# A fused two-block model on one core: attention takes its context pieces and its x pieces in turn

## The reference

```python
s = jnp.einsum('bikgd,bjkd->bkgij', q, kc).astype(jnp.float32) * (A_HEAD_DIM ** -0.5)
p = jax.nn.softmax(jnp.concatenate([sink_l, s], axis=-1), axis=-1).astype(vc.dtype)
return jnp.einsum('bkgij,bjkd->bikgd', p[..., 1:], vc).reshape(B, lc, A_WIDTH)
```

```python
s_loc = jnp.where(valid, s_loc, -jnp.inf)
s_ctx = jnp.einsum('bikgd,bjkd->bkgij', q_n, kc).astype(jnp.float32) * scale
p = jax.nn.softmax(jnp.concatenate([sink_l, s_ctx, s_loc], axis=-1), axis=-1).astype(v.dtype)
```

## Time and profile before

| what | value |
|---|---|
| median of 3 runs | 1845.88 us (1842.76 to 1850.29) |
| the profiled execution: time, span | 1848.1 us, 1845.4 us |
| TensorE (matmul), VectorE, ScalarE, GpSimd busy | 84%, 45%, 20%, 10% of the span |
| attention: first scores, first matmul of the output projection | 1312.58, 1383.15 us |
| granted TensorE clock in attention from 1319 us on | 1.00 |
| transfers in flight in attention, 1315 to 1380 us | share 0.00 to 0.01 |

### The profile page before, as it was taken

One profiled execution on the slowest core, in us unless ns is written; L12 is line 12 of the kernel. 1 busy time (PEld: TensorE's weight loads), 2 busy tenths in 40 slices (PEclk: granted clock), 3 DMA queues, 4 the chain that ended last, 5 costly groups with the idle time before them and its releaser, 6 DMA issues. The chain is left out here.

```text
span 1845.4 us, 19291 instructions
## 1 busy us (share of the span) xinstructions
PE 1555.1 (84%) x7431; PEld 933.9 (51%) x7431; DVE 826.0 (45%) x1536; ACT 371.3 (20%) x702; POOL 193.0 (10%) x282
## 2 busy tenths in 40 slices
PE   4999972689999799476799859999889799999877
PEld 2877662688444444242334325444564456646563
DVE  2344549344344377442112133355664325555553
ACT  3212153111101100110001010100450134622230
POOL 0000027300000000001000000000450001202330
PEclk8899976668999899678899979999899899999887
DMA  9221002210877476669999974252300221131101
GB/s 353 79 91 46 1 1 46 53 27 4 306 244 270 175 279 219 233 254 417 416 395 365 389 263 170 91 182 69 137 1 23 91 91 46 46 136 47 47 1 46
DMA packets 126745, 283.72 MB, mean 154 GB/s; under 512 B 28568, under 2 KB 30904, under 8 KB 121403
## 3 DMA queue, kind: packets, MB, share of 16 engines
q1 hardware_dynamic: 123056, 266.78, 39.5%
q0 software_dynamic: 3600, 15.73, 2.1%
HBM read 312.90 MB, written 4.19 MB: 172 GB/s over the span
## 5 line engine op out<-in xcount | busy, mean ns | idle before, releaser
L2245 PE MATMUL ps<-hT,ring 128*128 128x512 f32 x400 | 176.4, 600 | 0.3 <-issue 0.3
L1312 PE MATMUL ps<-ring,hTx 128*128 128x512 f32 x320 | 139.2, 593 | 1.9 <-PEq L178 1.8
L2245 PEld LDWEIGHTS ps<-hT,ring 128*128 128x128 f32 x400 | 76.7, 192 | 95.7 <-issue 95.5
L2588 PE MATMUL ps<-hT,ring 128*128 128x512 f32 x256 | 113.5, 600 | 3.1 <-PEq L2495 2.7
L299 DVE SCALAR_TENSOR_TENSOR ada_acc<-ring,cact,ada_acc 128x512 f32<-128x512 f32 x154 | 104.1, 746 | 0.5
L1312 PEld LDWEIGHTS ps<-ring,hTx 128*128 128x128 f32 x320 | 60.4, 190 | 77.1 <-issue 77.1
L603 PE MATMUL ps<-hTx,ring 128*128 128x256 f32 x384 | 90.9, 392 | 5.3 <-PEq L178 5.3
L2095 PE MATMUL ps<-ring,hT 128*128 128x512 f32 x192 | 86.4, 611 | 2.6 <-PEq L178 2.4
L603 PEld LDWEIGHTS ps<-hTx,ring 128*128 128x128 f32 x384 | 74.6, 197 | 19.6 <-issue 8.0
L2588 PEld LDWEIGHTS ps<-hT,ring 128*128 128x128 f32 x256 | 48.5, 192 | 62.0 <-issue 62.0
L1845 PE MATMUL ps<-ring,hTx 128*32 128x512 f32 x384 | 52.7, 699 | 24.7 <-DMA ring<-in_expert_w 24.7
(11 more groups left out here) (519 smaller groups left out, 2589.4 us busy)
## 6 DMA issues: line engine op xcount, KB each, us to landing
ring<-in_expert_w SPq DMA_DIRECT2D x24, 2048.0 KB, 14.5
far<-in_expert_w SPq DMA_DIRECT2D x24, 2048.0 KB, 18.0
ring<-in_w_in SPq DMA_DIRECT2D x16, 2048.0 KB, 13.5
ring<-in_ada_w SPq DMA_DIRECT2D x12, 2048.0 KB, 9.3
ring<-in_w_ada SPq DMA_DIRECT2D x12, 2048.0 KB, 8.8
ring<-in_w_in_c SPq DMA_DIRECT2D x10, 2048.0 KB, 7.7
ring<-in_expert_w POOLq DMA_DIRECT2D x32, 512.0 KB
far<-in_expert_w POOLq DMA_DIRECT2D x32, 512.0 KB
```

The source lines that it names most:

```text
L1312: ins = pe.matmul(ps[:, 2 + i % BANKS], hTx[:, kt, t * P:(t + 1) * P], stream.slot(n)[:, kt], start=(kt == 0), stop=(kt == KT - 1))
L2245: ins = pe.matmul(bank, slot[:, kt, c0:c0 + P], hT[:, kt], start=(kt == 0), stop=(kt == KT - 1))
L2588: ins = pe.matmul(bank, slot[:, kt, j % 4 * P:(j % 4 + 1) * P], hT[:, kt], **edge)
```

## The change

The list `work` is written in another order: for each tile index and head, first the context piece, then the x piece of the same head. Even places now hold context pieces and odd places x pieces. Since x pieces are no longer the last 16, the number of `biased` that is waited for is counted over the list, and the wait for `turned` in the softmax of an x piece is left out for the first four places. What each piece does is the same, and so are LAG, banks and slots.

```diff
-                    work = [(t, h) for t in range(2 * TT) for h in range(A_HEADS)]
+
+                    work = [(s * TT + t, h) for t in range(TT) for h in range(A_HEADS) for s in range(2)]
                     N = len(work)
 
-                    N_CTX = TT * A_HEADS
+                    n_biased = lambda i: sum(t >= TT for t, h in work[:i + 1])
                     n_keys = lambda t: 2 * L if t >= TT else L
...
-                                if 0 <= k < N_CTX:
+                                if k >= 0 and work[k][0] < TT:
                                     pe.wait_ge(summed, k + 1)
-                                elif k >= N_CTX:
-                                    pe.wait_ge(biased, k - N_CTX + 1)
+                                elif k >= 0:
+                                    pe.wait_ge(biased, n_biased(k))
...
-                                    dve.wait_ge(turned, i - BUF + 1)
+                                    if i >= BUF:
+                                        dve.wait_ge(turned, i - BUF + 1)
...
-                                    dve.wait_ge(biased, i - N_CTX + 1)
+                                    dve.wait_ge(biased, n_biased(i))
```

## The result

| | before | changed |
|---|---|---|
| median of 12 runs | 1844.88 us (1841.90 to 1850.38) | 1855.16 us (1851.28 to 1861.84) |
| ratio, 95% interval | 1 | 1.0055 (1.0042 to 1.0068) |
| profiled execution: time, span | 1848.1, 1845.4 us | 1854.92, 1852.6 us |
| first scores to first matmul of the output projection | 70.57 us | 78.18 us |
| span behind it | 462.25 us | 461.87 us |

The changed kernel is slower by 10.2 us by the ratio (7.7 to 12.5), and by 7.2 us from span to span. In the traces the attention stage holds all of it: +7.61 us, with the same start to 0.03 us and 0.4 us less behind it.

The account below looks back on a forecast made before the run. Latency around a loop of two iterations, not an engine, was taken to bound attention. Middle +5.3, start +2.9 and end -0.8 sum to +7.4 us: median 1853.3 us (+0.40%), 8-in-10 range 1849 to 1859, forecast's own 1850.5 to 1857.

Parts of the forecast that it names:

- The chain: Attention: scores, softmax, exponential, copy, outputs, next scores but one; 5.22 us for two x pieces, 2.90 for two context pieces.
- the two loops: Attention after the change: odd iterations' loop 4.56 us, even iterations' 3.56; a pair takes the longer, before 4.06.
- Middle: Attention from S(5) to S(31), the score products of pieces 5 and 31: 53.98 to 59.28 us, +5.3.
- Start: First attention pieces, two of the first four now x pieces at low clock: S(5), piece 5's scores, at 1322.0, +2.9 us.
- upper bound for a clock that rises later: At the beginning of attention: +4.5 us if TensorE's clock rises later than worked out.
- End: Last attention pieces: piece 30, now context, is scaled early and its output is shorter; -0.8 us (0 to -1.2).
- 0.5% bound: Whole kernel: 9.2 us, about what a measurement can tell from no change; slower begins at 1855.1 us.
- rival 1: TensorE in attention: granted clock falls to 1.2 GHz for a time; five pairs give 1859.8 us; chance 0.09.
- rival 2: Attention: loop from output over VectorE's gate to next x softmax binds; pair 4.9, total +11.8, 1857.7 us; chance 0.08.
- rival 3: Attention: the two loops share slack, pair stays at 4.06 us; about +2, 1848 us; chance 0.06.
- rival 4: Attention: an engine becomes the bound, TensorE's 3.78 or VectorE's 3.13 us a pair; faster, 1836 us; chance 0.05.

Follow-up runs that it names:

- the order of two and two: Kernel before with two context pieces, then two x pieces in turn in the work list: 1846.31 us, ratio 1.0007.
- second and fourth sample: The changed kernel run again, nothing altered: ratio 1.0054 and attention 78.17 us, then ratio 1.0047 and attention 78.18 us.
- the later outputs on the changed order: Changed kernel with outputs and gates one iteration later: 1842.79 us, ratio 0.9974.
- third sample: The changed kernel run again, nothing altered: ratio 1.0057, attention 79.30 us.

## Why the prediction was right, and by how much not

**The loop.** The chain was read right: 5.22 and 2.90 for two pieces before, 4.56 for a mixed pair, found once in the trace before and then in the changed trace thirteen times. That the maximum of the two loops rules and not their mean is shown from three sides: the order of two and two brings 4.06 back, 0.37 us of added work costs nothing in the one loop and all of itself in the other, and with LAG 4 the pair takes 5.72 at full clock, the loop of x with x. That it is latency is shown by the additional iteration in the loop, which takes the bound away.

**The terms.** Middle +5.3: measured 59.28 - 53.98 = 5.30. Start +2.9: S(5) at 1322.01 where 1322.0 was worked out, with the stage's start 0.03 earlier, 2.93. That is not luck, since the steps between fit as well: the first two x exponentials stand at 1317.15 and 1320.15 (1317.2 and 1320.1 worked out), the first copy at 1321.06 (1321.05), its outputs at 1321.46 (1321.45). The upper bound for a clock that rises later wasn't needed: in the second and fourth sample it rose 6 us after the first scores and not 3, and S(5) still came 9.47 and 9.46 after them. End -0.8: 8.40 for 9.02 (the last gate before stood at 1382.11), -0.62. The last scaling ends 0.34 earlier (0.4 worked out), but from there to the last gate only 0.28 is saved and not 0.45: TensorE now waits 0.23 for the copy before the last outputs. Together 7.61, forecast 7.4; the end is the only term that was off, by 0.2 us.

**The total.** The forecast was 1853.3 and +0.40%; the medians say 1855.16, +0.55% (0.42 to 0.68). It lies in the forecast's own range of 1850.5 to 1857, but past the 0.5% bound, which the interval takes in; I had given "slower" 0.36 and "within" 0.58. All four ratios (1.0047 to 1.0057) lie above 1.0041, which the stage alone would give, though three of their four intervals take it in; their mean, 1.0053, is 9.8 us. Of the 2.2 us between, the clock at the start explains little: it cost 1.1 us in one of four profiled executions, 0.3 on average. The kernel before, run once more, came out 0.9 us above itself with a stage 0.07 shorter, and the order of two and two 1.3 above with 0.34 in the stage; both are within their intervals, and both show a gap of 1 us between ratio and trace that mixing one by one didn't make (the later outputs on the changed order show 0.6 the other way). For the rest I have no place; six traces show none outside the stage, with a scatter of 3 to 4 us that could hide it. It stays open. The step that the runs don't bear out is thus the last: that the median would move by what the traced stage moves. The executions in which the clock falls back at the start had no term in the sum; it would have been about 0.3 us.

**The rivals.** The clock (rival 1) did not come in the middle, where 1.00 held over ten pairs, but it came at the start in the third sample. What I had set against it, that no idle gap would be longer than the 1.24 us that the trace before passed at 1.00, doesn't protect: there TensorE's longest gap between the clock's rise and its fall was 0.96 us. The second loop (rival 2) has its slack: gate to x softmax never binds, VectorE waits 0.57 us for the scores each time. A stage at the mean (rival 3) is what the order of two and two gives, not this one. An engine as the bound (rival 4) needs the loop to be longer by an iteration first. The Trainium skill ("Perfetto Trace Analysis", Optimization Strategy) says that performance may be improved by interleaving regimes whose most contended engine differs. This case's runs show no such gain. Latency bound both regimes here, and not an engine: interleaved one by one the stage is 7.6 us slower, and two by two it is the same within 0.4 (70.91 for 70.57).

## What to carry to other kernels

When a stage in software pipeline runs at a pace that no engine's work explains, write down the loop: from an instruction through the queues back to its like, and over how many iterations it spans. If the order of unlike pieces is changed, take for each loop the pieces that meet in it; loops that always meet the same kind make the pace the maximum, loops that meet all kinds in turn make it the mean. And before reordering try one iteration more between the end of the loop and its beginning: here that was worth 8.8 us of the stage, for six changed lines.

## What the runs showed of the hardware that was not expected

The granted clock of TensorE can fall back just after it has risen. In the third sample of the changed kernel, at the stage's start:

```profile
1322.00:1324.00 2.00, 0.93 (x6) 0.42 (x4) 1.74 (x7) 0.95 (x4) 1.78 (x2) 1.00 0.00 0
1325.00:1328.00 3.00, 3.00 (x10) 1.86 (x10) 1.12 (x3) 0.43 (x1) 1.17 (x1) 0.50 0.00 0
1329.00:1334.00 5.00, 4.14 (x27) 3.04 (x25) 3.53 (x14) 2.82 (x10) 2.82 (x3) 1.00 0.00 0
```

TensorE had worked about half of the two microseconds at 1.00 (2.4 GHz), then ran at 0.50 (1.2 GHz) and fully busy for some 3 us, and came back. The wait of those 2 us, the longest between rise and fall:

```profile
1323.23 0.66 PE L334 MATMUL ps<-consts,up 128*128 128x128 f32 x4 [0.96 <-POOL up L2491]
```

The first trace of the changed kernel has the same instructions on TensorE and as much idle time (1.02 of 2.00 busy, 1319 to 1321) and kept 1.00, through a gap of 1.54 us too. In that trace the clock had risen earlier; but in the second and the fourth it rose as late as in the third (1321 to 1322) and kept 1.00 as well. Equal work gave two outcomes, for a difference of 1.1 us in the stage. With 2.17 us of idle time in each pair (LAG 4 on the changed order) the clock went up and down through the whole stage.
